# Identity products put into TensorE's waits, in a two-layer diffusion backbone with mixture of experts

## The reference, cut to what matters

```python
def expert_choice_ffn(h, w_router, w_gate, w_up, w_down):
    b, n, d = h.shape
    cap = CAPACITY_FACTOR * n // N_EXPERTS
    logits = jnp.einsum('bnd,de->ben', h, w_router).astype(jnp.float32)
    affinity = jax.nn.softmax(logits, axis=1)
    gates, idx = lax.top_k(affinity, cap)
    xs = jax.vmap(lambda hb, ib: hb[ib])(h, idx)
    ...
```

## Time and profile before

| | |
|---|---|
| median of 3 runs | 2136.82 us (2134.91 to 2136.83) |
| the profiled execution | 2138.91 us |
| its span, first to last instruction | 2137.1 us |
| mean granted clock of PE | 0.978 |
| PE busy | 1964.0 us, 92% of the span |
| DVE, ACT, POOL busy | 664.1, 532.1, 161.3 us |
| moved by DMA | 515.66 MB, 240 GB/s over the span |

### The profile page before, as it was taken

How to read it: one execution, slowest core, us unless ns; L and a number is a source line. 1 busy time by engine, 2 the same in 40 slices (tenths; PEclk the granted TensorE clock), 3 DMA queues, 4 the chain that set the end, 5 groups by cost and what they waited for, 6 DMA issues and landing times. The chain is left out here.

```text
span 2137.1 us, 27257 instructions
## 1 busy us (share of the span) xinstructions
PE 1964.0 (92%) x10872; PEld 927.1 (43%) x10872; DVE 664.1 (31%) x1744; ACT 532.1 (25%) x1224; POOL 161.3 (8%) x157
## 2 busy tenths in 40 slices
PE   6999989999979999999999899989997998888875
PEld 3446455556642332323323556455554333333322
DVE  3322345666650100101001632366665011020203
ACT  3111154555530000100100421165554110000001
POOL 1101010000010010020100101000000000000001
PEclk9999989999989999999999999999999999999999
DMA  9832020000199999999999402030007999999995
GB/s 365 305 137 82 2 78 1 1 2 1 40 354 411 422 364 417 379 390 419 364 414 421 157 20 79 8 91 1 21 24 273 373 426 427 426 426 427 427 427 247
DMA packets 90935, 515.66 MB, mean 241 GB/s; under 512 B 10594, under 2 KB 15628, under 8 KB 36540
## 3 DMA queue, kind: packets, MB, share of 16 engines
q1 hardware_dynamic: 84496, 493.29, 57.1%
q0 software_dynamic: 4416, 15.21, 2.4%
q10 hardware_dynamic: 1900, 5.43, 0.6%
HBM read 498.69 MB, written 15.20 MB: 240 GB/s over the span
## 5 line engine op out<-in xcount | busy, mean ns | idle before, releaser
L756 PE MATMUL psS<-arena 128*64 128x512 f32 (+9 forms) x4552 | 1158.3, 556 | 70.7 <-DMA arena<-in_w_up 20.7
L756 PEld LDWEIGHTS psS<-arena 128*64 128x64 f32 (+4 forms) x4552 | 455.5, 158 | 667.3 <-issue 587.7
L2041 DVE TENSOR_REDUCE mx<-psS 128x1 f32<-128x768 f32 (+2 forms) x200 | 165.5, 827 | 151.9 <-PE psS L756 149.9
L1352 ACT ACTIVATE arena<-psT 128x768 f32<-128x768 f32 (+7 forms) x261 | 150.1, 577 | 243.7 <-PE psT L759 230.2
L1352 ACT ACTIVATE arena<-psS 128x128 f32<-128x128 f32 (+5 forms) x158 | 61.8, 420 | 575.7 <-PE psS L756 530.6
L759 PE MATMUL psT<-ident,arena 128*128 128x128 f32 (+1 forms) x1036 | 172.4, 290 | 35.3 <-ACT arena L1352 9.3
L2225 DVE TENSOR_TENSOR arena<-arena,psS 128x512 f32<-128x512 f32 x32 | 20.6, 684 | 550.5 <-PE psS L756 550.5
L759 PEld LDWEIGHTS psT<-ident,arena 128*128 128x128 f32 (+1 forms) x1036 | 119.9, 144 | 134.3 <-issue 96.3
L756 PE MATMUL psT<-arena 128*32 128x512 f32 x1536 | 174.5, 595 | 0.0
L1352 ACT ACTIVATE arena<-psS,nb 128x768 f32<-128x768 f32 (+2 forms) x200 | 157.9, 792 | 1.4
L756 PE MATMUL psM<-arena 128*128 128x512 f32 x288 | 140.9, 611 | 0.0
(11 more groups left out here) (232 smaller groups left out, 1265.4 us busy)
## 6 DMA issues: line engine op xcount, KB each, us to landing
arena<-in_w_gate SPq DMA_DIRECT2D x117, 1024.0 KB, 14.6
arena<-in_w_up SPq DMA_DIRECT2D x116, 1024.0 KB, 18.7
arena<-in_w_down SPq DMA_DIRECT2D x116, 1024.0 KB, 26.0
arena<-in_w_mod SPq DMA_DIRECT2D x48, 1024.0 KB, 7.5
arena<-in_w_in SPq DMA_DIRECT2D x6, 2048.0 KB, 7.8
arena<-in_w_out SPq DMA_DIRECT2D x8, 512.0 KB, 7.8
arena<-in_w_out SPq DMA_DIRECT2D x2, 2048.0 KB, 15.2
normed_rows<-arena ACTq DMA_DIRECT2D x8, 512.0 KB, 7.3
```

The lines of the kernel that those rows point to most:

```text
L756: return nc.tensor.matmul(o, lhsT, rhs, start=start, stop=stop)
L1352: return nc.scalar.activation(o, i, f, **kw)
L2041: link(V.reduce_max(mx[:, par:par + 1], view(S, 0, P, 0, (512, 2), (1, n)), axis=AX.XY))
```

## The change

A helper issues `n` products of the 128 x 128 identity with itself into 128 columns of a bank that nobody reads there. It is called in three places: after each of the modulation chunks 4 to 7 (8 products) and after the transposes of the modulation row (14); in the second layer between the gate products and the wait for their copies (40); and in both layers ahead of the transposes of the gathered rows (24 in the first layer, 28 in the second).

```diff
+            def keep_busy(n, b, col=384):
+
+                for _ in range(n):
+                    mm(bank(b, col=col, w=P), ident[:, :], ident[:, :])
+
             def features(a, x):
...
                 if l == 0:
                     for n in range(KD // 2, KD):
                         mod_mult(n)
+                        keep_busy(8, 3)
                     mod_transpose(0)
+                    keep_busy(14, 3)
...
                 affinities(1)
                 gates(5, "fg", (0, 1, 2, 3))
                 late = range(MOD_FRONT * KD, (MOD_FRONT + 1) * KD) if l == 0 else ()
+                if l:
+                    keep_busy(40, 6)
                 for n in late[:6]:
                     late_mod(n)
                 pe.wait_ge(z["fgev"], 4 * l + 4)
...
                 for g in (MOD_FRONT,) if l == 0 else ():
                     mod_transpose(g, late_bank(g))
+                keep_busy(28 if l else 24, 6)
```

## The result

The changed kernel takes 2142.26 us in the median of 16 runs, the kernel before 2138.45 us in 16 runs on the same chips: a ratio of 1.0018, with a 95% interval of 1.0011 to 1.0025. It is slower by some 3.8 us (2.4 to 5.3), where 3.4 us were forecast.

The account below looks back on a forecast made before the run. TensorE was taken to bound the stretch from 40 us and the first layer's experts, the weight stream the second layer's. Front 2.1, first-layer rows 0 and lists 1.3 sum to +3.4 us on 2136.82: 2140.2 us, range 2135.0 to 2142.5.

Parts of the forecast that it names:

- the lists: Second layer, ahead of the list transposes: 40 products cost 8.8 us against a 7.3 us wait, so 1.3 us later.
- the front: Modulation chunks and row: 32 + 14 products start the transposes 3.42 us later, full clock returns 1.34: 2.1 us later.
- The rows of the first layer: Ahead of the gathered rows' transposes: 24 products cost nothing; the first expert product can start up to 1.2 us earlier.
- The price of a product: All places: one filling product costs 0.22 us, as two records of 0.11 us, with bounds 0.214 and 0.234.
- Rival (a): All places: a product costs 0.45 us, from unhidden weight loads or a low clock; some 2160 us; 9%.
- Rival (b): All places: cheaper products fit the waits and delay nothing, winning 1.34 us in front and 0.08 in lists; 2135.4 us; 17%.
- the pace of a chunk: Front, from chunk 4 on: PE needs 0.86 + 1.76 = 2.62 us a chunk, against arrivals 2.49 us apart.
- The term for the clock: Front, transposes and the projection's start: full clock instead of low gives 1.34 us back.
- PE is the bound behind it, so this stays: Behind the front: PE sets the pace, so the 2.1 us delay lasts to the end.
- the wait for the stream near 707 us: First layer's experts: PE waits 1.28 us for a weight chunk at 707.36; an earlier PE would wait longer there.
- a full clock gives nothing because the stream holds the layer: Second layer's gathered rows: 16 transposes run at full clock after 28 products, gaining nothing, since the weight stream sets the pace.
- Rival (c): All three places: the clock's gain reaches the end and products are free, 5.6 us faster, 2131.2 us; 7%.

Follow-up runs that it names:

- e2: Changed kernel with only the 40 products ahead of the second layer's list transposes, none in the other places: 2140.39 us, ratio 1.0012 to the kernel before.
- e6: Changed kernel with the front doubled (16 products behind each of four chunks, 28 behind the row's transposes): 2151.21 us, ratio 1.0067 to the kernel before.
- e7: Changed kernel with 64 products instead of 24 ahead of the first layer's gathered rows: 2149.59 us, ratio 1.0059 to the kernel before.
- e1: Changed kernel with only the products in front (8 behind each chunk, 14 behind the row's transposes): 2138.38 us, ratio 1.0004 to the kernel before.
- e3: Changed kernel with only the products ahead of the gathered rows (24 and 28): 2138.85 us, ratio 1.0005 to the kernel before.
- e4: Changed kernel with counts cut to the waits: 0, 5, 6, 4 and 10 in front, 30 ahead of lists, 16 and 20 ahead of rows: 2139.41 us, ratio 1.0006.
- e5: Changed kernel with 80 products instead of 40 ahead of the second layer's list transposes: 2150.06 us, ratio 1.0064 to the kernel before.
- e8: Changed kernel with 40 products instead of 28 ahead of the second layer's gathered rows: 2144.67 us, ratio 1.0031 to the kernel before.

## Why the prediction was right, point by point

**The total and its make-up.** 3.8 us were measured and 3.4 forecast. The time itself, 2142.26 us, lies 0.24 us inside the upper end of the range (2142.5); the forecast of 2140.2 stood on a median of 3 runs that is 1.6 us below that of 16, so that the time fell inside the range is luck in part. In the traces the end behind the lists is later by 1.9 us where 1.3 were forecast (by 1.7 in the mean of the changed kernel, e2, e6 and e7, all with the 40, against before, e1, e3 and e4, without them or with 30). For the front, the five profiled executions with 8 and 14 products (the changed kernel, e1, e5, e7, e8) begin the second section between 97.76 and 100.14 us, 98.8 in the mean; the three without products in front (before, e2, e3) between 96.53 and 97.51, 96.9 in the mean: 2.0 us later, where 2.1 were forecast. The rows of the first layer cost nothing, as forecast.

**The price of a product, 0.22 us.** Measured 9.03 us for 40 between their start and the next instruction, 0.226 us each, and 0.248 us where 8 stand between chunks (24.48 to 26.46). The first is within the bounds, the second a little over the upper one. Rival (a) is out: loads and matmuls overlap, although all these products use the same rows of the array, as the row of the loads beside the 40 shows (PEld is the weight load):

```profile
1645.28 8.90 PEld L756 LDWEIGHTS psO<-ident 128*128 128x128 f32 x79 [0.24 <-issue]
```

The rule of the Trainium skill (TensorE: Matmul & The Clock Gate, Part 3: Packing small matmuls) that a load overlaps a running matmul only if their row groups differ does not hold here. The other condition of rival (a), a low clock under the products, did occur ahead of the gathered rows: 24 in 6.6 us, 0.275 each. Rival (b) fell with the 0.226.

**The front.** The four chunks took 2.98 us each, with 2.62 forecast, and yet chunk 7 began at 32.42 (forecast 32.56) and the transposes at 38.87 (38.70). That agreement is luck in part: chunk 4 began at 23.48 instead of 24.70, since the first transposes ran at full clock in this execution. In e1 the clock was 0.72 from 22 to 24 us, and the transposes began at 39.80. From the start of chunk 4 to the transposes it is 15.4 us in all five executions with these products, where 14.0 were forecast. The term that was too small is the pace of a chunk, 2.62 us: its own products took 1.0 us instead of 0.86, and the eight fillers 1.98 instead of 1.76.

The term for the clock, 1.34 us, was right: from 3.59 us at the transposes the delay fell to 2.24 at 44.47, and it fell by 1.34 or 1.35 us in the other four executions too. But this gain only makes good a part of the fillers' own delay. It is not there to be won for itself: e4 shows that nothing of it is left where TensorE is on time, since the last tokens then hold it at 43.45.

The step that failed in the mechanism is "PE is the bound behind it, so this stays". It was read off a busy share of 9.81 of 10 us from 40 us on, but in this stage PE also waits, for tokens at 43.46 and for a chunk at 59.44, and in the changed kernel these waits took up 1.06 of the 2.24 us (0.15 to 1.02 us in the other four). So the products cost more than forecast, and part of the delay was taken up behind them. The two errors are of opposite sign, and in the mean of the executions the sum came out right: that is luck.

**The rows of the first layer.** The forecast had 24 products in 5.3 us and the experts up to 1.2 us earlier; the products took 6.6 us, because the clock was 0.50 when they began, and the experts began 1.1 us later. In the changed kernel:

```profile
627.00:628.00 1.00, 1.00 (x6) 0.50 0.96 393
628.00:629.00 1.00, 1.00 (x7) 0.50 0.96 393
```

The products were to keep the clock up and paid first to bring it up. That this costs nothing was right: the last combining products come at the same distance. The reason given, that it goes into the wait for the stream near 707 us, is not shown: this wait is shorter in the changed kernel (1.28 before, 0.62 at 704.87), but in e1 and e2, without products there, it is 0.58 and 0.56. e7 shows where the cover ends.

**The lists.** 1.85 us late, where 1.3 were forecast: the products cost 0.2 us more than forecast, and they began later behind the gate products, which took 5.24 us instead of 4.96 because the clock came up later in this execution. That the delay goes through to the end in full was the step that mattered, and e5 shows it with 8.7 us of 8.9. The statement that a full clock gives nothing because the stream holds the layer was too wide: PE earlier gives nothing, but e8 shows that PE later soon costs, and in e1 the end came 0.8 us later behind a first group at half the clock.

Rival (c), gains of the clock in all places, would have needed a place in which PE alone is waited for. The advice of the Trainium skill (TensorE: Matmul & The Clock Gate, Why this matters for your kernels) to leave TensorE no long gaps was followed here in three places, and no run here shows a gain from it: e4, whose counts were meant to delay nothing, has a ratio of 1.0006 (0.9994 to 1.0018).

## What to carry to other kernels

A higher clock for TensorE is worth something only where what follows waits for TensorE alone: before filling a wait, look one wait further, at what the work behind it will wait for. A filler is queued ahead of the real work, so it must end before the shortest wait that any execution shows, priced at the clock at which it starts; what is over is paid, in full where a gather and a weight stream hang on the next instruction (the lists), and not at all where the work behind has room for it (24 products ahead of the first layer's rows), until that room is used up (64). A stage in which the engine is busy for 98% of the time can still hold waits that take up a delay. Where a total can move by no more than a few microseconds of thousands, distances between two instructions of one execution help where the totals of many runs leave a question open; but they scatter too (by 0.8 us from the lists to the end, with the same code there), so take them from several executions, or make the effect larger.

## What the runs showed of the hardware that was not expected

Whether TensorE starts a short stretch at full or half clock differs between executions of the same code. Ahead of chunk 4 the clock from 22 to 24 us was 0.50 in the profiled executions of the kernel before and of e2, and 1.00 in those of e3 and the changed kernel. Without products this did not move the start of the transposes ahead of the projection (35.28, 35.51 and, at full clock, 35.98), because chunks from memory set the pace (TensorE waited 1.2 to 1.4 us for each of the last ones). With products the chain hangs on TensorE from 20 us on, and it did: 38.56 and 38.87 at full clock (e7, the changed kernel), 39.80 to 40.33 where the clock was low (e1, e5, e8).

The first layer's attention, in which nothing was changed, differed by 3.8 us between the two profiled executions, in the three stretches with the lower clock, more than the whole change is worth.
